# Expert weights through a ring of 16 places instead of 12, four experts a turn of the loop, and four spare places used once

## The reference, cut to what matters

```python
def moe_ffn(h, expert, gate, w_gate, w_up, w_down):
    ...
    def expert_block(args):
        xblk, e = args
        return (jax.nn.silu(xblk @ w_gate[e]) * (xblk @ w_up[e])) @ w_down[e]
    ...
x = layer_norm(ALPHA * x + att, ln1_g[layer], ln1_b[layer])
expert, gate = route(h, w_router, b_router)
ffn = moe_ffn(h, expert, gate, w_gate[layer], w_up[layer], w_down[layer])
x = layer_norm(ALPHA * x + ffn, ln2_g[layer], ln2_b[layer])
```

## Time and profile before

| | before |
|---|---|
| median of 3 runs | 2798.08 us (2797.85 to 2803.94) |
| the profiled execution: time, span | 2798.51 us, 2796.7 us |
| mean granted TensorE clock | 0.987 |
| PE busy, PE weight load busy | 2599.5 us (93%), 2008.1 us (72%) |
| DVE busy, ACT busy | 1274.0 us (46%), 836.0 us (30%) |
| moved by DMA | 685.17 MB, mean 245 GB/s |
| on the chain that ended last | PE 69%, DMA 20%, DVE 6% |

### The profile page before, as it was taken

The page is one execution under the profiler, slowest core; times in us unless marked ns, Lnnn a source line. Parts: engine busy times, 40 slices in busy tenths (PEclk is TensorE's granted clock), DMA queues, the critical chain, the costliest instruction groups (busy, mean ns, idle before and its releaser), DMA issues.

```text
span 2796.7 us, 46123 instructions
## 1 busy us (share of the span) xinstructions
PE 2599.5 (93%) x19503; PEld 2008.1 (72%) x19503; DVE 1274.0 (46%) x1875; ACT 836.0 (30%) x1051; POOL 0.2 (0%) x4
## 2 busy tenths in 40 slices
PE   8899888879899888879999999999999999999998
PEld 8743433348543333369999899999899898899998
DVE  4610101037411000055566765655655658766555
ACT  4300000025210000033343442443433444523433
POOL 0000000000000000000000000000000000000000
PEclk9999999999999999999999999999999999999999
DMA  8689999973899999955563441455555544323553
GB/s 270 264 357 425 426 425 425 426 286 106 329 400 425 425 425 425 426 192 181 181 230 122 135 140 59 137 166 181 181 181 181 192 152 150 107 77 107 166 181 136
DMA packets 286519, 685.17 MB, mean 245 GB/s; under 512 B 11992, under 2 KB 217616, under 8 KB 236944
## 3 DMA queue, kind: packets, MB, share of 16 engines
q1 hardware_dynamic: 282792, 671.27, 63.6%
q10 hardware_dynamic: 3560, 11.45, 1.1%
HBM read 681.63 MB, written 1.05 MB: 244 GB/s over the span
## 4 chain that ended last, share of the span: by engine, by line
PE 69%; DMA 20%; DVE 6%; ACT 2%; issue 1%; DVEq 1%; SPq 0%; ACTq 0%; POOLq 0%
PE psum L419 68%; DMA weight_ring<-in_w_gate 14%; DMA weight_ring<-in_w_up 3%; DMA weight_ring<-in_w_down 2%; DVE weight_ring_parts L2066 1%; PE psum L427 1%; ACT weight_ring_parts L2058 1%; DVEq L552 1%; DMA weight_ring<-in_w_in_a 0%; DVE arena L3260 0%; SPq L1921 0%; DMA h_tok<-in_mem 0%; DMA weight_ring<-in_w_in 0%; DVE arena L1837 0%; DVE small L2778 0%
## 5 line engine op out<-in xcount | busy, mean ns | idle before, releaser
L419 PE MATMUL psum<-weight_ring_parts,arena_parts 128*128 128x256 f32 (+1 forms) x2992 | 666.4, 315 | 6.3 <-DVE arena_parts L2159 1.9
L2066 DVE TENSOR_TENSOR weight_ring_parts<-weight_ring,weight_ring_parts 128x2048 fp32r<-128x2048 f32 x217 | 496.5, 2290 | 338.0 <-ACT weight_ring_parts L2058 332.0
L419 PE MATMUL psum<-x_chan_parts,weight_ring_parts 128*128 128x256 f32 x3200 | 612.2, 282 | 12.9 <-DVE arena_parts L2155 7.7
L2058 ACT ACTIVATE weight_ring_parts<-weight_ring 128x2048 fp32r<-128x2048 f32 x217 | 414.9, 1913 | 465.7 <-POOLq L532 345.4
L419 PE MATMUL psum<-weight_ring,arena 128*64 128x512 f32 (+1 forms) x2112 | 474.8, 582 | 73.8 <-DMA weight_ring<-in_w_gate 39.1
L419 PEld LDWEIGHTS psum<-weight_ring_parts,arena_parts 128*128 128x128 f32 x2992 | 496.4, 189 | 42.9 <-issue 3.3
L419 PEld LDWEIGHTS psum<-x_chan_parts,weight_ring_parts 128*128 128x128 f32 x3200 | 509.0, 190 | 18.3 <-issue 12.9
L419 PE MATMUL psum<-arena 64*64 64x64 f32 (+7 forms) x4616 | 467.0, 335 | 29.3 <-DVE arena L1837 15.6
L419 PEld LDWEIGHTS psum<-weight_ring,arena 128*64 128x64 f32 (+1 forms) x2112 | 179.3, 140 | 361.4 <-issue 358.5
L419 PE MATMUL psum<-weight_ring_parts,x_chan_parts 128*128 128x256 f32 x2336 | 427.5, 285 | 2.3 <-DVE arena_parts L2155 2.2
L419 PE MATMUL psum<-arena_parts,weight_ring_parts 128*128 128x256 f32 x1536 | 419.0, 283 | 0.0
(11 more groups left out here) (324 smaller groups left out, 1713.6 us busy)
## 6 DMA issues: line engine op xcount, KB each, us to landing
weight_ring<-in_w_gate SPq DMA_DIRECT2D x92, 1024.0 KB, 23.2
weight_ring<-in_w_up SPq DMA_DIRECT2D x92, 1024.0 KB, 22.9
weight_ring<-in_w_in SPq DMA_DIRECT2D x70, 1024.0 KB, 5.0
arena<-in_w_down SPq DMA_DIRECT2D x64, 1024.0 KB, 22.5
weight_ring<-in_w_down SPq DMA_DIRECT2D x64, 1024.0 KB, 23.2
weight_ring<-in_ffa_w_in SPq DMA_DIRECT2D x44, 1024.0 KB, 7.1
weight_ring<-in_ffb_w_in SPq DMA_DIRECT2D x44, 1024.0 KB, 5.7
arena<-in_w_gate SPq DMA_DIRECT2D x36, 1024.0 KB, 18.5
```

The costliest lines, as they stand in the source:

```text
L419: return nc.tensor.matmul(*args, **kw)
L2058: nc.scalar.activation(HIGH[buf], ring[:, sl, :], ACT.Copy).then_inc(s_hi, 1)
L2066: nc.vector.tensor_tensor(ring_parts[:, sl, :], ring[:, sl, :], f32(HIGH[buf]), ALU.subtract).then_inc(s_split, 1)
```

## The change

- The expert ring has 16 places. The order changes too: places 0 to 7 are the weight ring, 8 to 11 the four in the arena, 12 to 14 the three arena places that `FIRST_ROWS` had, 15 is `XT`.
- Four spare places are read once in each layer: two in the arena where the first pair's activations (`SILU`, `HG`, `HT`, `YD`) will be written (gate j = 3), one behind table 1 in `tables`, which is 512 columns longer (down j = 0, expert 0), and one in `GB` once ln1's gain and bias are read (down j = 0, expert 1, after the new semaphore `s_gained`). The decay bias rows `W0B` of the second block move to the end of `tables`.
- SP issues the set for `tables` first, before the wait for the arena.
- ln2's gain and bias are loaded after the first pair.
- The first pair's down and the second pair's gate and up are written out; the loop then takes two pairs a turn, so it has half as many turns, three where there was one pass.
- `Stream.load` waits for expert place s for its ring place s.

```diff
-EXPERT_SLOTS = 12
+EXPERT_SLOTS = 16
+SPARES = 4
...
-        C = sb("tables", [P, NC])
+        C = sb("tables", [P, NC + 512])
...
-                self.wait_slot(() if self.before is None else (EXPERT_SLOTS - SLOTS + s,))
+                self.wait_slot(() if self.before is None else (s,))
...
+        EXPERT_ROWS = [ring[:, i, :].rearrange("p (k n) -> p k n", n=D) for i in range(SLOTS)] + \
+            [view(at, 2, D) for at in (13568, 15616, 17664, 19712, 0, 8960, 11008)] + \
+            [XT.rearrange("p c n -> p (c n)").rearrange("p (k n) -> p k n", n=D)]
+        table_end = max(hi for _, hi in c1_at.values())
+        SPARE_ROWS = [view(work, 2, D), view(work + 2 * D, 2, D),
+                      C[:, table_end:table_end + 2 * D].rearrange("p (k n) -> p k n", n=D), GB[:, :, :]]
...
-            return en.e.snap(more * PAIRS + (PAIRS - 1))
+            return en.e.snap(more * (PAIRS // 2) + (PAIRS // 2 - 1))
...
             pe.e.wait_ge(s_v2p, pe.c["v2p"].next())
-            rest(begin([gather(0), gather(1)]), 0)
-            loops(pe, l, later_pairs(pe), lambda i: rest(down(False)))
-            down(True)
+            rest(begin([gather(0), gather(1)]), True)
+            rest(down(first=True))
+
+            def body(i):
+                for _ in range(2):
+                    rest(down())
+
+            loops(pe, l, later_pairs(pe), body)
+            down(last=True)
...
-            s_load_gb(a["ln2_g"][l], a["ln2_b"][l], D)
...
-            loops(s, l, later_pairs(s), lambda i: pair(False))
+            pair(False)
+            s_load_gb(a["ln2_g"][l], a["ln2_b"][l], D, wait=False)
...
             v_gain_and_bias(4 + 4 * l)
+            v.sync()
+            nc.vector.nop().then_inc(s_gained, 1)
...
             nc.vector.nop().then_inc(s_free[b], 1)
-            nc.vector.nop().then_inc(s_v2a, 1)
...
+            spare(2, "w_down", 0, 0)
+            sp.e.wait_ge(s_room, l + 1)
+            for sl in range(SLOTS, SLOTS + 4):
+                first_turn(sl)
+            for sl in range(SLOTS):
+                sp.wait_slot((sl,))
+                first_turn(sl)
 
             sp.e.wait_ge(used, old.size + old.n)
...
+            spare(0, "w_gate", 0, 3)
+            spare(1, "w_gate", 1, 3)
+            for sl in range(SLOTS + 4, EXPERT_SLOTS - 1):
+                first_turn(sl)
+            sp.e.wait_ge(s_gained, l + 1)
+            spare(3, "w_down", 1, 0)
+            sp.e.wait_ge(s_routed, l + 1)
+            first_turn(EXPERT_SLOTS - 1)
+            down(0, 2)
+            gate_and_up(1)
             steps = later_pairs(sp)
             with sp.e.Fori(0, steps) as i:
                 sp.enter(f"moe{l}", (i, 1))
-                down(sp.e.snap(i & (PAIRS - 1)))
-                for j in range(4):
-                    gate_and_up(sp.e.snap((i + 1) & (PAIRS - 1)), j)
+                for k in range(2):
+                    down(later_pair(sp, i * 2 + (1 + k)))
+                    gate_and_up(later_pair(sp, i * 2 + (2 + k)))
             sp.leave(steps)
             down(PAIRS - 1)
```

More of the change, by code:

```diff
@@ L594, in build @@
         lay = Layout(after_mem)
[L595 to L598, removed]
         XG, PM, PG, PGT = lay(KC, P), lay(T, P), lay(T, P), lay(SEQ)
+        work = lay.at
         SILU, HG, HT, YD = lay(2, 2 * BLK), lay(D), lay(KC, P), lay(D)
+        EXPERT_ROWS = [ring[:, i, :].rearrange("p (k n) -> p k n", n=D) for i in range(SLOTS)] + \
[4 more added lines that the diff above has]
+                      C[:, table_end:table_end + 2 * D].rearrange("p (k n) -> p k n", n=D), GB[:, :, :]]
         LSUM, MX, NMX, RCP = (tiny(DIL_HEADS, T) for _ in range(4))
@@ L861, in v_gain_and_bias, with s_load_gb @@
                 nc.vector.tensor_tensor(X[:, t, :], X[:, t, :], GB[:, 1, :], ALU.add)
-        def s_load_gb(gain, bias, n):
-            s.e.wait_ge(s_v2a, s.c["v2a"].next())
+        def s_load_gb(gain, bias, n, wait=True):
+            if wait:
+                s.e.wait_ge(s_v2a, s.c["v2a"].next())
             for j, x in enumerate((gain, bias) if bias is not None else (gain,)):
@@ L1570, in two_pieces, with step @@
                 return opened
-            def step(j, opened, act, first=None):
+            def step(j, opened, act, spare=None):
                 rows = []
                 for e in range(2):
-                    if first is None:
+                    if spare is None:
                         slot = pe.job()
@@ L1580, in step @@
                     else:
-                        pe.e.wait_ge(s_first[first + e], 16 * (l + 1))
-                        rows.append(FIRST_ROWS[first + e])
+                        pe.e.wait_ge(s_spare[spare + e], 16 * (l + 1))
+                        rows.append(SPARE_ROWS[spare + e])
                 for kk in range(2):
@@ L1614, in begin, with rest @@
                 return gate, gathered[1]
-            def rest(begun, ahead=None):
+            def rest(begun, first=False):
                 gate, second_half = begun
@@ L1623, in rest, with down @@
                         read(second_half)
[L1624 to L1628, removed]
+                    step(j, gate, XG, 0 if first and j == 3 else None)
+                    step(j, up, XG)
+            def down(last=False, first=False):
                 up_piece = pe.pieces.n - 2
@@ L1648, in down @@
                 for j in range(4):
-                    step(j, opened, HT)
+                    step(j, opened, HT, 2 if first and j == 0 else None)
                 gate = None if last else begin(gathered)
@@ L1711, in s_moe, with body @@
             s.skip()
-            loops(s, l, later_pairs(s), lambda i: pair(False))
+            pair(False)
+            s_load_gb(a["ln2_g"][l], a["ln2_b"][l], D, wait=False)
+            def body(i):
+                for _ in range(2):
+                    pair(False)
+            loops(s, l, later_pairs(s), body)
             pair(True)
@@ L1870, in v_moe, with body @@
             evict(flat(XG[:, 4:8, :]))
-            loops(v, l, later_pairs(v), lambda i: pair(i, False))
+            pair(0, False)
+            def body(i):
+                for k in range(2):
+                    pair(i * 2 + (1 + k), False)
+            loops(v, l, later_pairs(v), body)
             pair(PAIRS - 1, True)
@@ L1875, in g_moe, with steps_done, down @@
             g.skip(6 + 2)
-            def steps_done(n):
-                for _ in range(n):
+            def steps_done(n, spare=0):
+                for i in range(n):
                     g.e.wait_ge(s_half, g.c["half"].next())
+                    if i < spare:
+                        continue
                     g.jobs.n += 2
                     g.e.sem_inc(s_used, 2)
-            def down(last):
+            def down(last=False, spare=0):
                 g.skip(4 if last else 6)
-                steps_done(3)
+                steps_done(3, spare)
                 g.freed(2, 2)
@@ L1893, in g_moe @@
             steps_done(6)
-            g.skip(4)
+            g.skip(2)
+            g.freed(2, 2)
+            down(spare=1)
+            gate_and_up()
             def body(i):
-                down(False)
-                gate_and_up()
+                for _ in range(2):
+                    down()
+                    gate_and_up()
             loops(g, l, later_pairs(g), body)
-            down(True)
+            down(last=True)
         def sp_moe(l):
@@ L1915, in one @@
                 src = rows_of_expert(w, e, j, pr)
[L1916 to L1920, removed]
+                sp.wait_slot()
                 sp.e.dma_start(EXPERT_ROWS[sl], src).then_inc(s_slot[sl], 16)
[L1923 to L1926, removed]
@@ L1928, in down, with gate_and_up @@
-            def down(pr):
-                for j in range(4):
+            def gate_and_up(pr):
+                for j in range(4):
+                    for w in ("w_gate", "w_up"):
+                        for e in range(2):
+                            one(w, e, j, pr)
+            def down(pr, first=0):
+                for j in range(first, 4):
                     for e in range(2):
                         one("w_down", e, j, pr)
-            for j in range(3):
-                gate_and_up(0, j)
@@ L1936, in sp_moe, with spare @@
-            sp.e.wait_ge(used, old.size + old.n)
[L1937 to L1942, removed]
+            def spare(i, w, e, j):
+                sp.e.dma_start(SPARE_ROWS[i], rows_of_expert(w, e, j, 0)).then_inc(s_spare[i], 16)
+            turn = [(w, e, j) for j in range(3) for w in ("w_gate", "w_up") for e in range(2)] + \
+                [("w_up", e, 3) for e in range(2)] + [("w_down", e, 1) for e in range(2)]
@@ new lines, in sp_moe, with first_turn @@
+            for _ in turn:
+                sp.jobs.take()
+            def first_turn(sl):
+                sp.e.dma_start(EXPERT_ROWS[sl], rows_of_expert(*turn[sl], 0)).then_inc(s_slot[sl], 16)
+            spare(2, "w_down", 0, 0)
[5 more added lines that the diff above has]
```

(2 more changed lines are left out.)

30 lines of the change are left out of this document (17 added, 13 removed).

## The result

| | before | after |
|---|---|---|
| median of 5 runs | 2798.23 us (2797.85 to 2803.94) | 2783.69 us (2781.14 to 2788.16) |
| ratio to before | | 0.9941 (95% interval 0.9928 to 0.9954) |
| the profiled execution: time, span | 2798.51, 2796.7 us | 2781.14, 2779.3 us |
| expert stage of layer 0: SP's first issue into the arena to TensorE's last down step | 99.15 to 593.47, 494.3 us | 98.71 to 584.02, 485.3 us |
| the same of layer 1 | 705.31 to 1197.33, 492.0 us | 695.66 to 1180.55, 484.9 us |

The forecast was 2784.0 us, with a range of 2778 to 2793. Two more comparisons of the same kernel gave 0.9955 (0.9938 to 0.9972) and 0.9946 (0.9933 to 0.9960). The two profiled executions lie 17.4 us apart: 9.0 us of it in layer 0's expert stage, 7.1 in layer 1's, and 1.3 spread over the rest.

What follows compares the result with a forecast made beforehand. Each expert stage ends when its DMA stream ends. Gains of 6.2 us (layer 0), 3.6 (layer 1) and 4.9 (early sets), 14.7 less 0.2, take 14.5 from 2798.5: 2784.0 us, range 2778 to 2793.

Steps and rivals of the forecast that it cites:

- Part 1: Expert 0's first quarter of down rows, issued before the arena wait into empty DMA engines: 4.9 us gained over both layers.
- Parts 2 and 3: More sets before first return of places: 4.9 us; 16-place ring: 1.8 of layer 0's second 3.1 us pause left.
- Part 4: Broadcast loads at the first pair's end, 1 MB in the full stream: bytes already counted, no further cost.
- Parts 5 and 7: Loops of two pairs, one pair written out; next stage's first loads some 10 us sooner: no gain or cost.
- Part 6: One more drain and nop on DVE, one nop less, before the first gather: 0.1 us cost in each layer.
- A: DMA pace falls with 14 sets in flight instead of 10; a 1% loss is 8.8 us: 2792.8; chance 0.08.
- B: SP held up in longer straight code, two or three stops of 1 to 2 us per layer: 2791; chance 0.12.
- C: PE fetches the doubled loop body anew each turn; at 23 us a stop 27 us slower, 2826; chance 0.05.
- D: Last rows and next stage's earlier loads share engines, up to 18 us at each stage end: 2820; chance 0.03.

Runs made afterwards that it cites:

- the second run: The changed kernel measured again with nothing altered: layer 0 443.3 us from TensorE's first gather, layer 1 483.8 us from SP's first issue into the arena.

## Why the prediction was right

**The bound** was read rightly: the stage ends when its stream ends. It ended 9.0 and 7.1 us sooner, and the rest of the program took 1.3 us less, not more. That the median of 2783.69 lies 0.3 us from the forecast is luck: the interval is 3.6 us to either side, and the two traces lie 17.4 us apart where 14.5 were forecast, 1.6 of the difference in the two stages.

**Part 1, the early set, failed in layer 0.** It was booked at 2.5 us there; the run without it showed 0. A pause that ends with a return of places, not with bytes, swallows whatever was sent ahead of it. The sum stayed right because the set in line would have filled the same pauses whose rest I had subtracted: 1.3 and 1.8 us were booked as cost in the same layer. In layer 1, where no pause is left, the run gave 1.3 to 2.4 us against 2.5, with a scatter of 1.1.

**Parts 2 and 3** had their times right. The queue ran dry at 150.9 (forecast 151.4) and at 187.0 (187.6 to 188.4); the losses were 1.6 and 2.2 us for 1.3 and 1.8; SP's return after the lull stood at 187.98 for 188.88, since TensorE's first gather came 1.0 us sooner (141.64). Their shares were not additive: the ring alone (with the late ln2 load in it) gives 4.4 us by the lengths of both stages, the spares with the ring of 12 nothing, both together 15.5 to 16.1. The spares supply sets to bridge the lull only if the ring can also take more returns before it, and the ring's room is worth little with the first pause 10 us long. In numbers, when the last pause of layer 0 ends, 28 sets were in before, 34 now, and SP's issue that ends it comes 3.5 us later after the first gather (46.3 for 42.8); 6 x 2.47 - 3.5 = 11.3 us, with the ln2 load of 2.5 us still to come: 8.8 us, measured 8.4 from the gather and 9.0 from the first issue.

The same count puts four kernels of layer 0 in order: time from gather to that issue, plus 2.47 us for each set still out, plus 2.5 where the ln2 load is still to come. The gathers start at 142.63, 141.64, 142.78 and 143.33 us, the issues at 185.44, 187.98, 152.02 and 193.46.

| | issue after gather | sets in | count | measured |
|---|---|---|---|---|
| before | 42.8 | 28 | 447.9 | 450.8 |
| changed | 46.3 | 34 | 439.1 | 442.4 |
| ring of 16, no spares | 9.2 | 16 | 446.4 | 449.5 |
| spares, ring of 12 | 50.1 | 32 | 447.8 | 451.9 |

The measured lengths are 2.9 to 4.1 us above the count each time.

**Layer 1** gave 7.1 us (8.2 in the second run) where 6.0 was forecast. What was left out is likely that the stretch before the first pause ran at 413 GB/s (727 to 756.5) and now at 426 (720 to 747): 30 us x 3% is 0.9 us. The ln2 loads lay in that stretch before and do not now. This was not tried by itself, and the scatter of 1.1 us is as large.

**Part 4**: leaving the ln2 load out saves 1.1 to 1.5 us of its 2.5 in layer 0, and the cut load comes with a dip of its own, in which sets were waiting in the queue; the full price lies between that and the 2.5 us. In layer 1 it is not settled. **Parts 5 and 7** at nothing: borne out by the loop alone and by the late next-stage loads, although the next stage's first loads are issued 29 us sooner than before (563.10 for 592.27), not 10. **Part 6** at 0.2 us was not separated: from the end of gain and bias to the first gather it is 10.5 us before and 9.9 after, and TensorE's ten counting matmuls in between, 2.1 and 1.3 us at different clocks, hide it.

**The rivals.** A fell: 426 GB/s at 26 us from issue to landing. B fell: the loop alone cost no whole time that can be measured, and SP's issues from 157.74 to 168.04 follow each other by the same 3.43 us as before. C's packets came and cost nothing: PE still waits for rows in the loop, by 1.3 us at a time. The Trainium skill ("Runtime: NRT & Kernel Launch", Instruction fetch mechanics) says that a taken branch to a target outside the pages held has to fetch it first; the 3 to 4 packets that appear between 250 and 580 us once the body is twice as long fit that. Whether any engine stopped for one, no run here shows. D fell: with the next stage's loads held back, the last step did not come sooner than in a run of the changed kernel. The sum of the rivals' chances for "slower" was added up wrongly: C, D and others make 0.10, not 0.08. The 358 GB/s that the Trainium skill ("DMA: Bandwidth & Descriptors", Specifications) gives for one core are passed by 19% for 330 us in the kernel after too. In its section on measured bandwidth (Bandwidth, Measured) that page of the Trainium skill gives about 358 GB/s to each core when both cores of the pair stream, and here one core ran.

## What to carry to other kernels

In a stage that ends with its DMA stream, add up nothing that lies before the last pause: count the sets that are in when that pause ends, and when it ends. Then ask which instruction ends it. Buffers read once prefetch more but return nothing, so give them to the reads whose return is needed least, and check the lull in the returns before adding more of them.

## What the runs showed that was not expected

- Removing 1.05 MB from a stream that looked full (419 GB/s from 189.5 to 250 us) saved in layer 0 only about half of its 2.5 us: the rest came back as a dip near 200 us, while the small rest of the load was in flight and sets were waiting in the queue.
- The same kernel takes 42.9 or 45.6 us from SP's first issue to the first gather in layer 0, with a mean granted clock of 0.92 or 0.80 over that stretch, a mix of 2.4 and 1.2 GHz; TensorE has small router and zeroing matmuls and waits there. Since the pauses that follow end with TensorE's reads, these 2.7 us pass through to the end of the stage, though the stage is bound by DMA.
- Leaving out most of a norm's parameters made the kernel 470 us longer, by one more pass of all sets: the number of passes is data.
